# Hybrid decoder step on one core: the input projection in 44 halves, with the key units and the first value units between them

## The reference, cut to what matters

```python
mod = silu(c) @ w_ada + b_ada                       # 1024 x 6144: six parts, sh1 sc1 gt1 sh2 sc2 gt2
h = rmsnorm(x, g_pre1) * (1 + sc1) + sh1
hq, hf, hi, hg, aq, ak, av, ua, ub = split(h @ w_in)  # 1024 x 5632
o_a = hgrn2_recurrence(...)                         # gated linear recurrence, 4 heads, state 128 x 128
q, k = rope(aq), rope(ak)                           # 8 heads of 64
# moba_attend: a new token scores 2048 cached positions (16 pages of 128) in 8 blocks,
# keeps the 3 blocks with the largest q . mean(k), adds its own block, one softmax
o_b = moba_attend(q, [cached k, k], [cached v, v])
merged = sigmoid(ua) * (o_a @ w_proj_a) + sigmoid(ub) * (o_b @ w_proj_b)
x = x + gt1 * rmsnorm(merged @ w_out, g_post1)
h = rmsnorm(x, g_pre2) * (1 + sc2) + sh2
g_, u_ = split(h @ w_gu)                            # 1024 x 5632
x = x + gt2 * rmsnorm((silu(g_) * u_) @ w_down, g_post2)
```

## Time and profile before

| | us |
|---|---|
| median of 3 runs | 771.5 |
| lowest and highest run | 768.93, 771.68 |
| span of the profiled execution | 767.2 |
| TensorE busy in it | 654.4 |
| VectorE busy | 409.3 |
| ScalarE busy | 267.9 |
| GpSimd busy | 86.0 |
| mean granted clock of TensorE, share of full | 0.903 |

### The profile page before, as it was taken

How to read it: one execution, slowest core, us unless ns; L and a number is a source line. 1 busy time by engine, 2 the same in 40 slices (tenths; PEclk the granted TensorE clock), 3 DMA queues, 4 the chain that set the end, 5 groups by cost and what they waited for, 6 DMA issues and landing times.

```text
span 767.2 us, 13224 instructions
## 1 busy us (share of the span) xinstructions
PE 654.4 (85%) x5195; PEld 549.4 (72%) x5195; DVE 409.3 (53%) x496; ACT 267.9 (35%) x382; POOL 86.0 (11%) x110
## 2 busy tenths in 40 slices
PE   4769999999945767758989689973999999999995
PEld 1268999899933656534524259962999999999993
DVE  0552322425579979964368435649435353543526
ACT  1244323533472212121121333433546464532412
POOL 2050000000053265001111100002100000000000
PEclk9979999999985998965597979996999999999997
DMA  8876887685457978987597998631165546445301
GB/s 329 310 287 220 296 309 272 247 304 193 152 195 226 307 278 292 343 274 255 194 345 266 381 339 275 207 111 55 58 185 153 174 145 187 150 152 182 96 1 62
DMA packets 94257, 168.93 MB, mean 220 GB/s; under 512 B 6449, under 2 KB 37865, under 8 KB 91010
## 3 DMA queue, kind: packets, MB, share of 16 engines
q1 hardware_dynamic: 76562, 137.68, 52.3%
q10 hardware_dynamic: 14368, 19.86, 7.8%
q0 software_dynamic: 3280, 10.71, 3.6%
HBM read 163.51 MB, written 4.72 MB: 219 GB/s over the span
## 4 chain that ended last, share of the span: by engine, by line
PE 70%; DVE 14%; DMA 4%; ACT 4%; issue 3%; POOL 2%; ACTq 1%; SPq 0%; DVEq 0%
PE ps L1248 18%; PE ps L1250 17%; PE ps L1249 17%; DVE KT L939 3%; PE ps L1396 3%; PE ps L1259 3%; PE ps L1458 2%; DMA ring<-w_in 2%; DMA ring<-cache_v 1%; PE ps L1427 1%; DMA ring<-w_ada 1%; DVE hx L1096 1%; PE ps L1377 1%; PE ps L1303 1%; PE ps L1590 1%
## 5 line engine op out<-in xcount | busy, mean ns | idle before, releaser
L814 DVE TENSOR_TENSOR w_lo<-ring,w_hi 128x1024 fp32r<-128x1024 f32 (+1 forms) x128 | 152.2, 1216 | 148.4 <-ACT w_hi L479 148.3
L1248 PE MATMUL ps<-h_hi,w_hi 128*128 128x288 f32 x704 | 211.8, 301 | 19.1 <-POOL h_lo L386 19.1
L1249 PE MATMUL ps<-h_lo,w_hi 128*128 128x288 f32 x704 | 209.3, 297 | 0.0
L1250 PE MATMUL ps<-h_hi,w_lo 128*128 128x288 f32 x704 | 208.5, 296 | 0.0
L479 ACT ACTIVATE w_hi<-ring 128x1024 fp32r<-128x1024 f32 (+1 forms) x128 | 129.9, 1043 | 164.1 <-PE ps L1250 92.9
L1248 PEld LDWEIGHTS ps<-h_hi,w_hi 128*128 128x128 f32 x704 | 133.6, 190 | 26.8 <-issue 13.4
L1250 PEld LDWEIGHTS ps<-h_hi,w_lo 128*128 128x128 f32 x704 | 134.1, 190 | 0.0
L1249 PEld LDWEIGHTS ps<-h_lo,w_hi 128*128 128x128 f32 x704 | 133.8, 190 | 0.1
L939 DVE STREAM_TRANSPOSE KT<-ring 128x2048 f32<-128x2048 f32 x32 | 72.0, 2280 | 1.8 <-PE ps L1377 1.8
L1377 PE MATMUL ps<-KT,Wk 128*32 128x128 f32 x1024 | 41.0, 315 | 31.7 <-DVE KT L939 31.7
L1377 PEld LDWEIGHTS ps<-KT,Wk 128*32 128x32 f32 x1024 | 32.1, 126 | 40.4 <-DVE KT L939 27.1
(11 more groups left out here) (285 smaller groups left out, 850.7 us busy)
## 6 DMA issues: line engine op xcount, KB each, us to landing
ring<-w_ada SPq DMA_DIRECT2D x24, 1024.0 KB, 6.9
ring<-cache_k SPq DMA_DIRECT2D x96, 256.0 KB, 4.0
ring<-w_in SPq DMA_DIRECT2D x22, 1024.0 KB, 10.2
ring<-w_gu SPq DMA_DIRECT2D x44, 512.0 KB, 4.7
ring<-cache_v SPq DMA_DIRECT2D x64, 256.0 KB, 6.4
ring<-w_down SPq DMA_DIRECT2D x10, 1024.0 KB, 5.0
ring<-cache_k ACTq DMA_DIRECT2D x32, 256.0 KB, 3.8
ring<-cache_v ACTq DMA_DIRECT2D x32, 256.0 KB, 5.5
```

The lines of the kernel that those rows point to most:

```text
L814: dve.tensor_tensor(w_lo[:, par, k, :], slot4(s)[:, k, :], w_hi[:, par, k, :].bitcast(F32), ALU.subtract).then_inc(sem("lo_split"), 1)
L1248: pe.matmul(dst, h, x_hi, start=first, stop=False)
L1249: pe.matmul(dst, h, x_lo, start=False, stop=False)
L1250: return pe.matmul(dst, l, x_hi, start=False, stop=last)
```

## The change

The input projection becomes 44 halves, each with its own of three buffers (`dense_in`, `hi`, `lo`), and its groups come in the order queries, keys, forget gate, recurrence query, then the rest. Halves 8 to 43 (D), the 32 key units (K) and value units 0 to 15 (V) form one written order `SEQ`, which all engines follow; the recurrence, the key and value token copies and the softmax stand at named places in it. The ring's order is the list `ITEMS`: 11 rows of `w_ada` ahead of the first `w_in` item, then mixed. All pages are issued by SP. The softmax of the cached part is done in two groups of four sequences (`gate_sums`, `choose_blocks`, `max_spread`, `probs_sum`), the first between D25 and D36, the second between D41 and the first of the remaining value units. Value units 16 to 31, the recurrence's sample part and the prompt's attention follow. The last eight rows of `w_ada` (for the second norm) go to buffers of their own (`ada3`) and are multiplied between items 26 and 31 (`ada_late`). The masks of own positions, the buffers' places and the banks of the accumulator are moved accordingly; the state products' input `vms` is made by GpSimd instead of VectorE.

For VectorE the order at each D x is: transpose key unit x-7, then split half x+2. For SP it is, at an even x, `w_in` item x/2+1 and key unit x-7, at an odd x key unit x-7, and a value unit at each V.

The core of the diff:

```diff
-    A_SLOTS = [("ada", 0, k) for k in range(DT)] + [("in", 0, 0), ("in", 0, 1)]
-    for i in range(8):
-        A_SLOTS += [("ada", 1 + i // 4, 2 * (i % 4)), ("ada", 1 + i // 4, 2 * (i % 4) + 1), ("in", 1 + i, 0), ("in", 1 + i, 1)]
-    A_SLOTS += [("in", g, k) for g in (9, 10) for k in range(2)]
-    W_AT = [n for n, (kind, _, _) in enumerate(A_SLOTS) if kind == "in"]
...
+    GROUPS = (AQ, AK, HF, HQ, HI, AV, HG, UA, UA + 4, UB, UB + 4)
+    def mixed():
+        d, k, v = iter(range(8, 2 * NW)), iter(range(32)), iter(range(16))
+        seqs = ["DKDKDKDK"] * 5 + ["DKDVKDVKDVK", "DVKDVKDVKDVK", "DVKDVKDVKDVVK", "DVDVDVDV"]
+        take = {"D": d, "K": k, "V": v}
+        return [(c, next(take[c])) for c in "".join(seqs)]
+    SEQ = mixed()
+    ITEMS = [("A", k) for k in range(11)] + [("D", 0), ("D", 1), ("A", 11), ("A", 12), ("D", 2), ("A", 13), ("A", 14), ("D", 3), ("K", 0), ("D", 4), ("A", 15)]
+    for c, x in SEQ:
+        if c == "D":
+            ITEMS += [("D", x // 2 + 1)] * (x % 2 == 0 and x + 2 < 2 * NW) + [("K", x - 7)] * (x < 39)
+        elif c == "V":
+            ITEMS.append((c, x))
+    ITEMS += [("V", v) for v in range(16, 32)]
+    B0 = len(ITEMS)
+    BW = B0 - NW
...
+            def slot_free(n):
+                if n < NSLOT:
+                    return
+                kind, x = ITEMS[n - NSLOT]
+                if kind == "A":
+                    sp.wait_ge(sem("ada_used"), x + 1)
+                elif kind == "D":
+                    sp.wait_ge(sem("lo_split"), 2 * (x + 1))
+                elif kind == "K":
+                    sp.wait_ge(sem("key_slots"), x + 1)
+                else:
+                    sp.wait_ge(sem("value_slots"), x + 1)
...
+            def load_ada3(k):
+                if k == 0:
+                    sp.wait_ge(sem("st_stored"), 16)
+                elif k == 1:
+                    sp.wait_ge(sem("pa_scored"), AH)
+                    sp.wait_ge(sem("ds_done"), HH)
+                elif k < 4:
+                    sp.wait_ge(sem("st_stored"), 80)
+                else:
+                    sp.wait_ge(sem("ada_used"), 2 * DT + k - 3)
+                sp.dma_start(ada3[k % 4][:, :], inp["w_ada"][0, k * P:(k + 1) * P, 8 * BC:12 * BC]).then_inc(sem(f"ada3_landed{k % 4}"), 16)
...
+            def hi(hh):
+                w, half = hh // 2, hh % 2
+                n = RING["D", w]
+                if half == 0:
+                    act.wait_ge(sem(f"landed{n % NSLOT}"), landed(n))
+                if hh >= 3:
+                    act.wait_ge(sem("w_used"), hh - 2)
+                act.activation(w_hi[hh % 3][:, :, :], slot4(n % NSLOT)[:, 2 * half:2 * half + 2, :], ACT.Copy).then_inc(sem("hi_split"), 1)
...
+            def lo(hh):
+                w, half = hh // 2, hh % 2
+                n = RING["D", w]
+                dve.wait_ge(sem("hi_split"), hh + 1)
+                dve.tensor_tensor(w_lo[hh % 3][:, :, :], slot4(n % NSLOT)[:, 2 * half:2 * half + 2, :], w_hi[hh % 3][:, :, :].bitcast(F32), ALU.subtract).then_inc(sem("lo_split"), 1)
...
+            def turn_keys(u):
+                n = RING["K", u]
+                dve.wait_ge(sem(f"landed{n % NSLOT}"), landed(n))
+                if u >= 2:
+                    dve.wait_ge(sem("kt_used"), u - 1)
+                dve.transpose(KT[:, u % 2, :, :], ring[:, n % NSLOT, :].rearrange("p (g n) -> p g n", n=512)).then_inc(sem("key_slots"), 1)
...
+            for i, (kind, x) in enumerate(SEQ):
+                if kind == "D":
+                    if x - 7 < 32:
+                        turn_keys(x - 7)
+                    if x + 2 < 2 * NW:
+                        lo(x + 2)
...
+            def choose_blocks(g):
+                b4, c = slice(4 * g, 4 * g + 4), slice(32 * g, 32 * g + 32)
+                dve.wait_ge(sem("gate_sum"), g + 1)
+                link(dve.tensor_copy(gate[:, c], ps[:, (5, 4)[g], 0:32]))
+                g3 = gate[:, c].rearrange(bn, b=4)
...
+            def dense_in(hh):
+                w, half = hh // 2, hh % 2
+                g, k = w // 2, w % 2
+                products(w, half, hh % 3, h_hi, h_lo, 4 * k, k == 0, k == 1, "tile_done",
+                         free=("tile_out", 4 * g - 4) if g and k == 0 else None, need=("h_lo", 4 * k) if g == 0 else None)
...
+            def cached_keys(u):
+                b, j = u // 4, u % 4
+                bank = 4 + b % 2 if b < 4 else 4
+                if j == 0:
+                    pe.wait_ge(sem("wk_ready"), b + 1)
+                    if b == 1:
+                        pe.wait_ge(sem("k_tok"), 1)
+                    elif b >= 2:
+                        pe.wait_ge(sem("scores_out"), b - 1 if b < 5 else b)
+                    if b == 3:
+                        pe.wait_ge(sem("kept_s"), 1)
...
+            def values(v):
+                g, i = v // 16, v % 16
+                n = RING["V", v]
+                if i == 0:
+                    pe.wait_ge(sem("probs_ready"), 4 * g + 4)
+                    if g:
+                        pe.wait_ge(sem("om_ready"), 1)
+                    else:
+                        pe.wait_ge(sem("kept_s"), 2)
+                pe.wait_ge(sem(f"landed{n % NSLOT}"), landed(n))
+                for q in range(4):
+                    ins = pe.matmul(ps[32 * q:32 * q + 32, 5, :], Pt[:, 4 * g + q, i, :], ring[:, n % NSLOT, q * 512:(q + 1) * 512],
...
+            for kind, x in SEQ:
+                if kind == "D":
+                    dense_in(x)
+                elif kind == "K":
+                    cached_keys(x)
+                else:
+                    values(x)
...
-            between = {6: [turn_hgrn], 24: [hgrn_states]}
-            for gi in range(8):
-                between[8 + 2 * gi] = [lambda gi=gi: gram(gi)]
-            for u in range(4 * NSEQ):
-                cached_keys(u)
-                if u % 4 == 0 and u:
-                    restrip(u // 4 - 1)
-                for step in between.get(u, ()):
-                    step()
...
+            values(16)
+            sample_out(0)
...
+            def prompt_step(k):
+                if k < AH:
+                    pa_scores(k)
+                if 1 <= k <= AH:
+                    pa_turn(k - 1)
+                if 2 <= k <= AH + 1:
+                    pa_values(k - 2)
+            prompt_step(0)
+            values(17)
+            prompt_step(1)
+            values(18)
+            values(19)
+            prompt_step(2)
+            values(20)
+            for h in range(HH):
+                hgrn_sample_out(h)
+            values(21)
+            prompt_step(3)
+            values(22)
+            o_sum()
...
+            ada_late(0)
+            pe.wait_ge(sem("m_lo"), 2)
+            dense(27, 1, m_hi, m_lo, 4, False, True, "y1_done")
+            ada_late(1)
+            dense(28, 0, m_hi, m_lo, 0, True, False, "y1_done", free=("y1_out", 0))
...
```

More of the change, by code:

```diff
@@ L117, in build @@
     _, at = constants()
-    NCONST = max(e for _, e in at.values())
+    NCONST = at["pad"][1]
     FIRST = at["eps"][1]
@@ L1065, in sample_state @@
+            for b in range(4, 8):
+                turn_probabilities(b)
+            row_scales(1)
             def sample_state(h):
@@ L1267, in turn_ada @@
                 for j in range(4):
[L1268 removed]
+                    ins = pe.transpose(ps[:, TURN_BANK[g], j * P:(j + 1) * P], (arow, arow, arow3)[g][:, j * P:(j + 1) * P], ident)
                 ins.then_inc(sem("mod_rows_turned"), 1)
[L1271 to L1287 removed]
@@ new lines, in products @@
+            def products(w, half, buf, x_hi, x_lo, kts, first, last, done, bank0=0, free=None, rows=BK, need=None):
+                pe.wait_ge(sem("lo_split"), w * 2 + (half + 1))
+                if need is not None:
+                    pe.wait_ge(sem(need[0]), need[1] + (half + 1) * rows // 2)
+                for j in range(4):
+                    if free is not None and half == 0:
+                        pe.wait_ge(sem(free[0]), free[1] + (j + 1))
+                    for kt in range(half * rows // 2, (half + 1) * rows // 2):
+                        kb = kt - half * rows // 2
+                        ins = three(ps[:, bank0 + j, 0:T], (w_hi[buf][:, kb, j * P:(j + 1) * P], w_lo[buf][:, kb, j * P:(j + 1) * P]),
+                                    x_hi[:, kts + kt, :], x_lo[:, kts + kt, :], first and kt == 0, last and kt == rows - 1)
+                    if j == 3:
+                        ins.then_inc(sem("w_used"), 1)
+                    elif last and done and half == 1:
+                        ins.then_inc(sem(done), 1)
@@ L1289, in _, with dense @@
+            def dense(w, par, *rest, **more):
+                for half in range(2):
+                    products(w, half, 2 * par + half, *rest, **more)
+            def dense_in(hh):
[3 more added lines that the diff above has]
+                         free=("tile_out", 4 * g - 4) if g and k == 0 else None, need=("h_lo", 4 * k) if g == 0 else None)
             pe.wait_ge(sem("const0_landed"), 16)
```

1304 lines of the change are left out of this document (698 added, 606 removed).

## The result

The changed kernel takes 819.2 us (median of 4 runs, 817.57 to 820.42) against 770.2 us before, in the same session: ratio 1.0653, 95% interval [1.0608, 1.0698]. I had forecast 773 us, no change, with a range up to 808 us. The profiled execution has a span of 817.8 us, 49 us over the 768.7 of my sum.

A forecast was written before the change was run, and what follows sets the result against it. It took a VectorE and DMA loop, waiting for ring slots, to bound the mixed stages. From 767.2 us, 2.5 gained before the output projections and 4 lost behind made a 768.7 us span, so 773 us measured, no change; range 725 to 808.

The forecast's parts named there:

- Start: Beginning of the input projection: three more w_ada rows ahead; first half near 51 us instead of 45.3, half 8 about 86.
- Halves 10 to 27: First mixed stage: nine pairs of steps, each a VectorE and DMA loop of 11.9 us, plus 21 us: 128 us, to 226.
- 4.9 us for the load: In each pair's loop, a 1 MB ring item takes 4.9 us or a little more from issue to landing, nothing ahead.
- the side work: VectorE's other work in halves 10 to 27, not hidden in load waits: 21 us, bounds 10 and 38.
- I cost that move at nothing: All pages issued by SP alone: 4 x 0.33 us, hidden behind the 2.78 us of their transfer.
- Halves 28 to 39: Stage with value items, five ring items a pair: six pairs of 15 to 19.5 us, together 105 us, to 331.
- Halves 40 to 43: End of the projection: halves 12.5, units 8, output product and sums 4, second group's softmax wait 10 us; together 35.
- Tail: Value unit 16 to M, the output projections' first instruction: old stage's 78 us plus 9 for stalls; M at 453 us.
- Behind M: After the output projections' first instruction: eight w_ada rows move here; 4 us added, bounds 0 and 12.
- The load latency is hidden: Rival for the projection with key and value units: TensorE binds, 715 us; chance 0.24, wholly or in part.
- The clock falls between the halves: Rival for the mixed stage: waits lower TensorE's clock, a half takes 5.8 instead of 3.1 us; 787 to 810 us; chance 0.16.
- The range: Whole kernel: 725 to 808 us; side work, second group's wait and tail taken as independent, together -17 and +22 us.

The follow-up runs named there:

- one issue: Changed kernel with each key item loaded by one DMA instruction from four neighbouring pages: 813.4 us; with key and value items both loaded so: 810.0 us.
- key first: Changed kernel with only the ring's item order changed, to key, weight, key instead of weight, key, key in each pair of steps: 785.4 us.
- the run without key pages: Changed kernel whose 32 key items keep their ring slots and waits but load nothing: 788.0 us.
- leaving out the value pages: Changed kernel with the key ahead of the weight item in the ring, and value items 0 to 15 loading nothing: 766.4 us.
- the values' move: Changed kernel with the first 16 value units moved behind half 43: 814.0 us; with the key ahead of the weight item in the ring too: 779.6 us.
- the kernel of three edits: Changed kernel with key ahead of weight in the ring, a value unit between scores and turn, and first 16 value units behind half 43: 763.6 us.

## Why the prediction was wrong

The mechanism of the first mixed stage, a loop of VectorE and the key's load in the ring's order, was right and is shown; its load term was too small. Further on the sum also missed a second loop (the value item's) and the price of TensorE's own work at a lower granted clock in the tail. All these errors lie to the same side.

**Start: right.** Half 0 at 50.6 (forecast 51), half 8 at 87.4 (86), split of half 11 done at 100.8 (98).

**Halves 10 to 27: the step that failed is "4.9 us for the load".** VectorE reached the end of its ninth pair at 242.2 us: 141.4 us for the 128 I gave it. The loop edge runs from the end of the split to the start of the transpose, and in eight of nine pairs it took 5.4 to 7.1 us, mean 6.15, in the ninth 7.6. That is 56.8 us in place of 44.1, nearly all of the 13 us missing; transposes and splits (9 x 6.96) and the side work (22 us for my 21) were as worked out. I had taken issue to landing of one instruction, the shortest case on record. The hops on either side are not the difference: from the split to the first issue it is 0.16 us in eight of the nine pairs, and from the landing to the transpose mostly 0.02. The load itself is longer. With one issue it takes 5.4 to 5.8 us to land (once 6.6), and in the ring's order SP issues the next key and a weight item right behind it, 0.4 and 1.6 us later in the pair at 131 us, so it shares the way; that this sharing is the reason was not tested. "I cost that move at nothing", the page issues of SP, was a smaller error: 0.3 us a pair by the run with one issue. That the loop exists and lies in the order of the ring is shown by key first and by the run without key pages, which end at the same place. TensorE's share of a pair was too small as well, though it did not bind: with the loop gone ten pairs from half 8 to 28 take 136 us, 13.6 a pair, of which TensorE is busy for 12.0, where I had 11.

The Trainium skill, "DMA: Bandwidth & Descriptors", in its rules for kernel authors, says of loads spread over SP, ACT and GpSimd that this gives no bandwidth and only saves the sequencers' issue time. No run here spreads the loads again; on the issue time the runs with one issue agree, there was little to save (6 us with the keys in one issue, 9 with keys and values).

**Halves 28 to 39: a size, and a second loop left out.** I gave 105 us; from the end of half 27 to that of half 39 it took 116.0. The loop that I described is there: VectorE's pairs took 16.6, 20.1, 21.8, 20.8, 20.7 and 15.7 us, where I had 15, 17, three times 19.5 and 15, and its waits for the key behind a value and a weight item were 11.2 to 13.0 us from the third pair on, for my 10.5. But it is not alone. I had no loop through the value item's load and TensorE, and that one is as long: without key pages 115.0 us from half 28 to half 40 stay of 119.1, and with the key first it takes leaving out the value pages to come from 112.5 to 90.9. Even with key loads that cost nothing my 105 is not reached: by the ends of halves 27 and 39, as I had counted, that run has 109.0 us.

**Halves 40 to 43: right in sum.** 33.8 us (forecast 35), the second group's wait among them. In part this is luck: TensorE was busy for 27.4 us where my terms of work made 24.5, and idle for 6.4 where I had put 10.

**Tail: the step that failed is that its work was carried over at its old price.** I gave it 87 us with 9 for the stalls; it took 102.8. This is the stage of the kernel before that I took the term from:

```profile
347.50:455.40 107.90, 95.64 (x488) 43.07 (x488) 51.28 (x111) 24.88 (x63) 15.04 (x28) 0.75 0.85 298
```

Without 16 value units its work is 95.6 - 21.8 = 73.8 us, and my 87 left 13.2 us idle. In the changed kernel TensorE is busy for 85.1 us and idle for 17.8. So of the 16 us some 11 are the work, at a granted clock of 0.63 in place of 0.75, and 5 the idle time, in which the waits ahead of the turns (2.1 to 2.9 us each) stand with 16.0 us where I had put 9.

**Behind M: a size.** From M to the first half of the FFN 86.9 us against 80.3 in the earlier trace rows, 6.6 more where I had 4 (to the end of the span it is 7.7). By my estimate of 1.15 us a row about 3.5 are the three rows of w_ada between projection halves; the rest was not taken apart.

The sum of the misses, at TensorE: 20 up to the end of half 27 (16 of them at VectorE, 3 of these from the start), 11, -1, 16 and 4 us, 50 in all; the span missed by 49.

**The rivals.** *The load latency is hidden* was the thing to try, not the thing that is: it needed another ring order. *The clock falls between the halves* did not hold. Of halves 9 to 27 four took more than 4 us, and the 19 of them together 5.5 us more than 19 times 3.45, for a rival that asked 14 to 37. The granted clock was 0.89 there, and 0.97 once key first and the values' move had closed most of the waits. It was the tail where the clock cost something, and there I had not looked for it.

The Trainium skill, "TensorE: Matmul & The Clock Gate", section "HAM oscillation — how this bites in real kernels", has, for a kernel of short bursts, every burst behind a DMA wait start throttled. The trace agrees for a few halves only: halves 9, 16, 18 and 27 began with matmuls 0.24 us apart, for 1.8 to 4.2 us, and were at 0.13 before their end; the other 15 of halves 9 to 27 ran at 0.13 from their second matmul on.

**The range.** I had taken the misses as independent and let the spreads cancel. They were not: the first two are loops closed by a load that I had read at its shortest, and in the tail the work and the idle time came out longer together.

**Where the gain went.** The overlap does work once the ring lets it: in the kernel of three edits halves, keys and the second group's maximum are done from 51.0 to 307.2 us, 256 us, where projection, key units and softmax took 302 before. Of these 46 us, 33 are given back up to M (140.5 us against 107.9), 6 at the start, 6 behind M. The 33 are the same TensorE work as before at another clock, and more waits. The window is to be held against the one of the kernel before above:

```profile
307.20:447.70 140.50, 113.86 (x489) 45.69 (x489) 44.28 (x99) 32.90 (x69) 5.67 (x3) 0.60 0.77 255
```

TensorE is busy for 113.9 us at a granted clock of 0.60, where 488 instructions took 95.6 at 0.75: 18 of the 33 us. The other 14 are idle time, 26.6 us for 12.3, with waits for value pages of 18.2 us for 8.1. In the changed kernel the rest was lost too: before, VectorE turned keys back to back, with every page already there; interleaved, the four slots carry weights as well, each is released late, and every late release starts a load that nothing covers.

## What to carry to other kernels

In a ring that several consumers release, write down for each item which release lets it be issued and how long after that it is wanted; place the items in the order in which their slots come free, so that nobody waits for the load that it has just released itself. Price such a loop from the consumer's release to the consumer's next start, not by the shortest issue-to-landing time. And put a unit of independent work between a product and the step that needs another engine's answer to it; changing only which of the dependent steps comes first moves the wait. When a stage's work is carried over from an old profile, look at the granted clock of both: here it was worth more than the waits.

## What the runs showed of the hardware

From the release of a slot by VectorE to VectorE's next start on the loaded 1 MB it took 5.5 to 5.9 us with one DMA instruction (in seven of eight pairs, 6.6 in the other) and 5.4 to 7.1 us with four of 256 KB, though the four need 2.1 us to be issued: by the means, 6.15 against 5.8 us, all but some 0.3 us of that is hidden. Behind half 43, where value loads are queued, four instructions an item gave a value unit every 3.1 us and one instruction every 2.70 us. That run also loads four neighbouring pages and needs no page numbers, so the split alone is not shown to be the price. With fewer waits the granted clock of the mixed stage was 0.97 in place of 0.89, with the same matmuls, and that of the next one 1.00 in place of 0.85, there with 12 value units fewer between the halves. In the tail a value unit put into each wait went with 0.74 in place of 0.65, and TensorE's same instructions were busy for 10.3 us less.
